# Two transformer layers on one core: what is asked for first, and where the memory rows and bias rows stand

## The chip, the cores and the metric

The kernel runs on one core of a Trainium2 chip. The metric is the device time of one execution in microseconds (us), median of three runs. The engines named below are PE (matrix products), DVE (vector), ACT (scalar/activation), POOL (general) and SP (which here only asks for transfers). PE writes into 8 banks of an accumulator memory (`PS`); DVE and ACT read from it.

## The reference

Two layers over a sequence of 512 rows of width 1024. Only the start of layer one matters here:

```
h = rmsnorm(x, g_pre_mix)                       # x: 512 x 1024
proj = h @ w_in                                 # columns: cb, cc, cv, q, k, v, qm, ga, gb, gc
o = moba_attention(q, k, v, rel_bias)           # logits + bias by distance (32 buckets, 8 heads), softmax, @ v
y_c = memory_attention(qm, rmsnorm(mem, g_mem), w_mem_kv)   # mem: 256 x 1024
merged = sigmoid(ga) * y_a + sigmoid(gb) * y_b + sigmoid(gc) * y_c
x = x + rmsnorm(merged @ w_out); then a gated feed-forward part; then layer two (state space, attention, experts)
```

The norm of `x` comes before every product; the norm of `mem` is first used by the product `mk` (behind `q`, `k`, `v`). The bias by distance is first used by the logits of the attention.

## The kernel before

Each engine has one program, written in the order in which it runs; engines wait for each other on counters. Nothing is reordered by a planner, so the order in the code is the order on the engine.

**Weights.** `weight_plan` cuts the weights into chunks of 1 MB ([128, 2048] f32), two of them (`q` half 0 and 1) for the name `q`, two for `k` and so on. Chunks are numbered here 0, 1 (`q`), 2, 3 (`k`), 4, 5 (`v`), 6, 7 (`mk`). There are two landing places: chunk n may only be asked for when chunk n-2 has been emptied. A chunk of these names has two parts of width 1024; part 0 and 1 lie in chunk 0, part 2 and 3 in chunk 1, and so on. Each part is split in a high and a low half: ACT makes the high half (`one_hi`, L1919, fed by `highs`), DVE the low half (`one_lo`, L1109, fed by `lows`); a chunk is empty when the low half of its last part is made. A product of two such pairs takes three matmuls (L490, L491, L492). `upto(e, n)` makes all parts below n that aren't made yet; `ahead(name, j)` makes up to the part four behind the start of tile j. The high half of part i also waits until the tile of part i-4 has been computed. SP's program asks for chunks (`one_in`, L2568) in order, each as soon as its place is empty.

**The head.** SP asks for `x` in four blocks of 512 KB (L2579) and then for chunks 0 and 1. ACT asks for four tables (`cols`, `consts`, `rows`, `wsmall`, L2078 to L2081), POOL for the memory rows `mem` (L2404, 2 x 512 KB), `onehot` and `rel_bias`. For each 128 rows ACT takes the sum of squares (`squared`, L1928), POOL turns it into a scale (`norm`: L2370, then L2373, which needs `consts`), DVE scales the rows (`scaled`, L1119). PE turns the scaled rows (`turned`, L486: one bank for each of 8 column groups, N1 for `x`, NM for `mem`), ACT writes the high half (L1935) and DVE the low half (L1129).

In before the order on ACT is: squares of x (4), squares of mem (2), high halves of parts 0 to 3, turned N1, turned NM, `q` tiles. On DVE: scale x (4), scale mem (2), low halves of parts 0 to 3, turned N1, the bias copy (L1337, L1339), turned NM, `q` tiles. On PE: turned N1, the bias product (L705), turned NM, four `q` tiles, four `k` tiles, the `v` rows, then attention.

**Bias.** The bias product gives 8 rows of 512. When DVE has copied them to `BV`, POOL writes each 128 times to DRAM (`bvec`, L2412, 2.5 MB), asks for `gains`, and then reads skewed rows back (`skew`, L2421) for the logits.

**Banks.** `banks.take` hands out the 8 banks in turn; who takes one waits for whoever last read it.

Of the kernel before, what the change touches and what calls it, by code (L numbers as in the profile page):

```python
# [175 lines left out]
class Events:  # L176
# [12 lines left out]
    def tick(self, name, key=0, by=1):  # L189
        self.n[name] = self.n.get(name, 0) + by  # L190
        if self.made:
            assert self.value[name, key] == self.n[name], (name, key)
            return self.sem(name), by
        assert (name, key) not in self.value, (name, key)
        self.value[name, key] = self.n[name]
        return None, by

    def at(self, name, key=0):
        return (self.sem(name), self.value[name, key]) if self.made else (name, 0)
# [59 lines left out]
def two_layers(nc, dram, out):  # L259
    ctx = ExitStack()  # L260
    with ctx:
# [43 lines left out]
        def ps(key):  # L305
            return PS[:, banks.of.get(key, 0), :]
# [170 lines left out]
        def tensor(e):  # L477
            def turned(N, consts=False):
                for k in range(8):
                    b, was = banks.take((N.name, k), ("v_out", (N.name, "l", k)))  # L480
                    if was:
                        e.wait_ge(*at(*was))
                    e.wait_ge(*at("consts"))
                    for i in range(N.n):
                        e.wait_ge(*at("v_out", (N.name, "x", i)))
                        m = e.i.transpose(PS[:, b, 128 * i:128 * i + 128], N.xn[:, i, 128 * k:128 * k + 128], ident)  # L486
                    m.then_inc(*tick("acc", (N.name, k)))
# [6 lines left out]
            def tile(name, j, N, back, n=512):  # L494

                b, was = banks.take((name, j), back)
                if was:
                    e.wait_ge(*at(*was))
                e.wait_ge(*at("w_lo", (name, j)))
                wh, wl = (cut(w, 8) for w in halves(name, j))  # L500
                for k in range(8):
                    e.wait_ge(*at("v_out", (N.name, "l", k)))
                    m = product(PS[:, b, 0:n], (wh[:, k, :], wl[:, k, :]), (N.hi[k], N.lo[k]), k == 0, k == 7)
                m.then_inc(*tick("acc", (name, j)))
# [193 lines left out]
                tile(name, j, N3, ("v_out", ("cs", tix, 3)))  # L698

            turned(N1)  # L700
            b, was = banks.take("bias", ("v_out", "bv"))
            e.wait_ge(*at(*was)) if was else None
            e.wait_ge(*at("onehot"))
            e.wait_ge(*at("rel_bias"))
            e.i.matmul(PS[0:8, b, :], GB[0:32, 512:520], GB[0:32, 0:512], start=True, stop=True).then_inc(*tick("acc", "bias"))  # L705
            turned(NM)
            for name in ("q", "k"):
                for j in range(4):
                    tile(name, j, N1, ("v_out" if j % 2 else "a_out", (name, j)))
            rows("v", N1, 4, lambda i: ("a_out", ("v", i)))  # L710
            zipped(attention_1(), dense_1())
            for bi in (1, 2):
# [391 lines left out]
        def vector(e):  # L1104
# [12 lines left out]
            def scaled(N, i):  # L1117
                e.wait_ge(*at("p_out", (N.name, "r", i)))
                e.i.tensor_scalar(N.xn[:, i, :], N.src[:, i, :], N.ss(i), None, ALU.mult).then_inc(  # L1119
                    *tick("v_out", (N.name, "x", i)))  # L1120
# [17 lines left out]
            def projected(name, dst):  # L1138
                for j in range(4):
                    projected_one(name, j, dst)  # L1140
# [189 lines left out]

            for i in range(4):
                scaled(N1, i)
            for i in range(2):
                scaled(NM, i)
            lows.upto(e, 4)
            turned(N1)
            e.i.memset(BV[0:8, 512:640], NEG).then_inc(*tick("v_out", "neg"))  # L1337
            e.wait_ge(*at("acc", "bias"))
            e.i.tensor_copy(BV[0:8, 0:512], ps("bias")[0:8, :]).then_inc(*tick("v_out", "bv"))  # L1339
            turned(NM)  # L1340
            projected("q", QT)
            projected("k", KT)
            for u in range(4):
                ahead("v", u)
# [567 lines left out]
        def scalar(e):  # L1912
# [14 lines left out]
            def squared(N, i):  # L1927
                e.i.activation(N.xn[:, i, :], N.src[:, i, :], ACT.Square, accum_out=N.ss(i)).then_inc(  # L1928
                    *tick("a_out", (N.name, "s", i)))
# [14 lines left out]
            def projected(name, dst):  # L1944
                for j in range(4):
                    projected_one(name, j, dst)
# [131 lines left out]
            e.i.dma_start(CP, dram["cols"]).then_inc(*tick("cols", 0, 16))  # L2078
            e.i.dma_start(CC, dram["consts"]).then_inc(*tick("consts", 0, 16))
            e.i.dma_start(RR, dram["rows"].to_broadcast([128, NROW])).then_inc(*tick("rows", 0, 16))  # L2080
            e.i.dma_start(WS, dram["wsmall"]).then_inc(*tick("wsmall", 0, 16))  # L2081


            for i in range(4):
                e.wait_ge(*at(f"xin{i}"))
                squared(N1, i)
            for i in range(2):
                e.wait_ge(*at(f"mem{i}"))
                squared(NM, i)
            highs.upto(e, 4)  # L2090
            turned(N1)
            turned(NM)
            projected("q", QT)
            projected("k", KT)
            for u in range(4):
                ahead("v", u)
# [271 lines left out]
        def pool(e):  # L2368
# [31 lines left out]
                    norm(N, i)  # L2400


            for i in range(2):
                e.i.dma_start(MEMR[:, i, :], dram["mem"][128 * i:128 * i + 128, :]).then_inc(*tick(f"mem{i}", 0, 16))  # L2404
            e.i.dma_start(GB[0:32, 0:512], dram["onehot"]).then_inc(*tick("onehot", 0, 16))
            e.i.dma_start(GB[0:32, 512:520], dram["rel_bias"]).then_inc(*tick("rel_bias", 0, 16))
            for i in range(4):
                norm(N1, i)
            for i in range(2):
                norm(NM, i)  # L2410
            e.wait_ge(*at("v_out", "bv"))
# [151 lines left out]
        def sync(e):  # L2563
            def one_in(e, n):
                c = chunks[n]
                for was in c.free:
                    e.wait_ge(*at(*was))
                e.i.dma_start(area(c.place, 2048), dram["wpack"][SLOT[c.name], :, 2048 * c.half:2048 * c.half + 2048]).then_inc(  # L2568
                    *tick(f"w_in{c.slot}", n, 16))

            loads = Feed(one_in)

            def until(name, j):

                p = parts[PART[name, j] + 3]
                loads.upto(e, CHUNK[p.chunk.name, p.chunk.half] + 3)

            for i in range(4):
                e.i.dma_start(X[:, i, :], dram["x"][128 * i:128 * i + 128, :]).then_inc(*tick(f"xin{i}", 0, 16))  # L2579
            until("down4", 3)  # L2580
            e.wait_ge(*at("acc", ("n3", 7)))
            e.i.dma_start(WD, dram["wdt"]).then_inc(*tick("wdt", 0, 16))
            loads.upto(e, len(chunks))

            def gates_in(n):


                e.wait_ge(*at("acc", ("gu", n // 2 - 3) if n > 5 else ("oo", 3, 1)))
                if n == 5:
                    e.wait_ge(*at("v_out", "wts"))  # L2590
                    e.wait_ge(*at("v_out", "be"))
                w, n_ = area(GUs[n % 6], 4096), 4096 if n < 2 * END else 2048
                e.i.dma_start(w[:, 0:n_], wexp[n, :, 0:n_]).then_inc(*tick(f"gu{n % 6}", n, 16))

            def rest_in(n):
                w = area(GUs[n % 6], 4096)
                e.i.dma_start(w[:, 2048:4096], wexp[n, :, 2048:4096]).then_inc(*tick(f"gu_rest{n % 2}", 0, 16))

            def downs_in(n):
                if n > 5:  # L2600
                    e.wait_ge(*at("acc", ("dn2", n // 2 - 3, 1)))
                e.i.dma_start(area(DNs[n % 6], 2048), wexp[n, :, 4096:6144]).then_inc(*tick(f"dn{n % 6}", n, 16))

            for blk in range(NBLK):
                n, m = 2 * blk, 2 * blk + 1
                if blk == 2:

                    gates_in(n)
                    downs_in(n)
                    downs_in(m)  # L2610
                    gates_in(m)
                    continue
                gates_in(n)
                gates_in(m)
                if blk == END:
                    rest_in(n)
                    rest_in(m)
                downs_in(n)
                downs_in(m)
            overflow(e, sync_more, before_end)  # L2620
            for s in range(2):
                e.wait_ge(*at(f"scatter{s}", END - 1 - s))
            e.wait_ge(*at("acc", ("gu", END - 2)))
            for i in range(4):
                e.i.dma_start(YC[i], YA2[128 * i:128 * i + 128]).then_inc(*tick(f"yc{i}", 0, 16))
            for i in range(4):
                e.wait_ge(*at("v_out", ("oc", i, 1)))
                e.i.dma_start(out[128 * i:128 * i + 128, :], X[:, i, :]).then_inc(*tick(f"out{i}", 0, 16))
            for i in range(4):
                e.wait_ge(*at(f"out{i}"))  # L2630
# [260 lines left out]
```

## Time and profile before

| | us |
|---|---|
| median of 3 runs | 2213.04 (2212.13 to 2213.21) |
| profiled execution | 2212.32 |
| its span | 2210.2 |
| PE busy | 2021.2 (91%) |
| DVE busy | 993.7 (45%) |
| ACT busy | 699.5 (32%) |
| POOL busy | 218.8 (10%) |
| mean granted clock of PE | 0.969 |

The span is what the hardware profiler recorded from the first to the last instruction; the profiled execution took 2.1 us more than that. PE busy at 91% is a mean over stages: in the first 100 us of the span it stands still before the first product and is dense behind it.

### The profile page before, as it was taken

Reading aid. Unit: us, or ns where it says so; the run is one execution under the profiler, and the core shown is the slowest. Engines: PE = TensorE matmul, PEld = TensorE weight load, DVE = VectorE, ACT = ScalarE, POOL = GpSimd, SP = SyncE. Lnnn points to the kernel's source line nnn. Section 1 sums busy time; section 2 is a strip of 40 time slices with the busy share of each in tenths; the row PEclk is TensorE's granted clock in tenths of the full one; section 3 lists DMA queues with packets and bytes.
Section 4 is the critical chain, followed back from the end, with each engine's and each line's share of the span. In section 5 each row is a group of like instructions: output and inputs, shape, how many; then the busy total and the mean of one; then the engine's idle time right before and its main releaser. Section 6 shows DMA issues by size and latency. Waiting matters only on the chain.

```text
span 2210.2 us, 23020 instructions
## 1 busy us (share of the span) xinstructions
PE 2021.2 (91%) x9514; PEld 1406.4 (64%) x9514; DVE 993.7 (45%) x1558; ACT 699.5 (32%) x1120; POOL 218.8 (10%) x280
## 2 busy tenths in 40 slices
PE   6989999997999999899999999999995988888886
PEld 4867788896888788777777765666693332322232
DVE  4366534335666622668887426662236111111113
ACT  4343323324444412555554322552121110100100
POOL 1000000002000000101211102110023111111110
PEclk9999999998999999999999999999997999999999
DMA  6531223242222332232232222112229999999995
GB/s 188 137 129 62 76 77 108 83 153 105 96 96 95 111 118 95 105 124 68 91 115 95 91 76 77 58 58 76 77 96 368 413 423 423 424 424 420 417 414 224
DMA packets 57336, 380.42 MB, mean 172 GB/s; under 512 B 13424, under 2 KB 13680, under 8 KB 24336
## 3 DMA queue, kind: packets, MB, share of 16 engines
q1 hardware_dynamic: 38304, 339.23, 39.4%
q0 software_dynamic: 18352, 38.66, 5.7%
q8 instruction: 75, 1.23, 0.2%
q10 hardware_dynamic: 576, 1.05, 0.1%
q14 instruction: 29, 0.24, 0.0%
HBM read 376.20 MB, written 27.86 MB: 183 GB/s over the span
## 4 chain that ended last, share of the span: by engine, by line
PE 69%; DMA 18%; DVE 8%; ACT 3%; issue 1%; POOL 1%; SPq 0%; DVEq 0%; POOLq 0%; ACTq 0%
PE PS L490 17%; PE PS L492 16%; PE PS L491 16%; DMA AR<-in_wexp 16%; PE PS L1067 4%; PE PS L860 4%; PE PS L537 2%; DVE rf L1109 2%; DVE AR L1326 1%; PE PS L841 1%; ACT rf L1919 1%; PE PS L486 1%; PE PS L1090 1%; PE PS L893 1%; PE PS L925 1%
## 5 line engine op out<-in xcount | busy, mean ns | idle before, releaser
L490 PE MATMUL PS<-rf,rf 128*128 128x512 f32 (+1 forms) x1896 | 725.8, 383 | 18.2 <-DVE rf L1109 10.7
L492 PE MATMUL PS<-rf,rf 128*128 128x512 f32 (+1 forms) x1896 | 713.7, 376 | 0.0
L491 PE MATMUL PS<-rf,rf 128*128 128x512 f32 (+1 forms) x1896 | 713.0, 376 | 0.0
L1109 DVE TENSOR_TENSOR rf<-AR,rf 128x1024 fp32r<-128x1024 f32 (+1 forms) x210 | 268.4, 1285 | 396.1 <-ACT rf L1919 396.1
L490 PEld LDWEIGHTS PS<-rf,rf 128*128 128x128 f32 x1896 | 360.9, 190 | 91.4 <-issue 18.0
L491 PEld LDWEIGHTS PS<-rf,rf 128*128 128x128 f32 x1896 | 361.1, 190 | 64.9 <-issue 3.1
L492 PEld LDWEIGHTS PS<-rf,rf 128*128 128x128 f32 x1896 | 360.0, 190 | 64.3
L1919 ACT ACTIVATE rf<-AR 128x1024 fp32r<-128x1024 f32 (+1 forms) x210 | 229.0, 1101 | 304.6 <-PE PS L492 191.4
L1067 PE MATMUL PS<-AR 128*64 128x512 f32 x1024 | 267.6, 629 | 54.9 <-DMA AR<-in_wexp 53.2
L1067 PEld LDWEIGHTS PS<-AR 128*64 128x64 f32 x1024 | 82.0, 145 | 234.8 <-issue 157.6
L1864 DVE TENSOR_TENSOR AR<-AR,PS 128x256 f32<-128x256 f32 x32 | 13.5, 422 | 358.9 <-ACT AR L2359 358.9
L1090 PE MATMUL PS<-AR 128*64 128x512 f32 x512 | 116.9, 599 | 16.5 <-DVE AR L1868 16.5
L860 PE MATMUL PS<-AR 128*128 128x512 f32 x256 | 112.5, 595 | 0.0
L2359 ACT ACTIVATE AR<-PS 128x256 f32<-128x256 f32 x32 | 12.3, 383 | 296.7 <-PE PS L1067 296.7
L1090 PEld LDWEIGHTS PS<-AR 128*64 128x64 f32 x512 | 33.9, 137 | 79.0 <-issue 54.8
L860 PEld LDWEIGHTS PS<-AR 128*128 128x128 f32 x256 | 47.9, 190 | 56.8 <-issue 56.2
L1326 DVE SCALAR_TENSOR_TENSOR AR<-PS,AR 128x511 f32<-128x511 f32 (+2 forms) x72 | 53.8, 747 | 13.8 <-ACT AR L2071 12.1
L2516 POOL DMA_INDIRECT AR<-h2d,IA x32 | 32.7, 1022 | 272.1 <-PE PS L1076 252.4
L2365 ACT ACTIVATE AR<-PS 128x512 f32<-128x512 f32 x32 | 19.1, 597 | 127.0 <-PE PS L1090 127.0
L486 PE MATMUL PS<-AR 128*128 128x128 f32 x112 | 24.7, 382 | 36.6 <-DVE AR L1119 36.4
L537 PE MATMUL PS<-AR 128*128 128x512 f32 x128 | 56.2, 592 | 0.0
L1872 DVE COPY AR<-PS 128x512 f32<-128x512 f32 x32 | 22.1, 692 | 65.3 <-PE PS L1090 65.3
(324 smaller groups left out, 1826.2 us busy)
## 6 DMA issues: line engine op xcount, KB each, us to landing
AR<-in_wexp SPq DMA_DIRECT2D x62, 2048.0 KB, 35.9
AR<-in_wpack SPq DMA_DIRECT2D x123, 1024.0 KB, 5.1
AR<-in_wexp SPq DMA_DIRECT2D x68, 1024.0 KB, 38.1
AR<-acud POOLq DMA_DIRECT2D x16, 512.0 KB, 4.0
AR<-ya SPq DMA_DIRECT2D x4, 1024.0 KB, 8.1
bvec<-AR POOLq DMA_DIRECT2D x1, 2560.0 KB, 54.8
AR<-in_x SPq DMA_DIRECT2D x4, 512.0 KB, 8.3
AR<-bvec POOLq DMA_DIRECT2D x8, 256.0 KB, 3.0
```

What stands on the lines that cost most here:

```text
L486: m = e.i.transpose(PS[:, b, 128 * i:128 * i + 128], N.xn[:, i, 128 * k:128 * k + 128], ident)
L490: e.i.matmul(o, ws[0], xs[0], start=start, stop=False)
L491: e.i.matmul(o, ws[0], xs[1], start=False, stop=False)
L492: return e.i.matmul(o, ws[1], xs[0], start=False, stop=stop)
L537: m = e.i.matmul(PS[:, b, :], w[:, k, c:c + 128], src[:, k, :], start=k == 0, stop=k == kt - 1)
L860: m = e.i.matmul(PS[:, b, :], w[:, d, :], YT[:, d, :], start=d == 0, stop=d == 15)
L1067: m = e.i.matmul(PS[CAP * j:CAP * j + CAP, b, :], xt[:, k, CAP * j:CAP * j + CAP], w[:, k, :], start=k == 0, stop=k == 7)
L1090: m = e.i.matmul(PS[CAP * j:CAP * j + CAP, b2[hf], :], hd[:, q, CAP * j:CAP * j + CAP], w[:, q, 512 * hf:512 * hf + 512], start=q == 0, st ...
L1109: e.i.tensor_tensor(rounded(p.place + p.width, p.width), src, rounded(p.place, p.width).bitcast(F32), ALU.subtract).then_inc(*tick("w_lo", ...
L1326: e.i.scalar_tensor_tensor(out=y[:, q:512], in0=b[:, 0:512 - q], scalar=cp("conv_w", 24 * (3 - q) + tix), in1=y[:, q:512], op0=ALU.mult, o ...
L1919: e.i.activation(rounded(p.place, p.width), area(p.chunk.place + p.off, p.width), ACT.Copy).then_inc(*tick("w_hi", p.key))
L2516: e.i.indirect_dma_start(XB[:, s, :], None, dram["h2d"], bass.IndirectOffsetOnAxis(ap=IA[:, 128 + blk:129 + blk], axis=0), bounds_check=51 ...
```

## The change

- SP: x, then only chunk 0; chunk 1 is asked for when all four blocks of x have landed.
- ACT: `wsmall` and the squares of mem move behind turned N1; of the parts only part 0 is split before turned N1, parts 1 and 2 behind it.
- DVE: only part 0 is split before turned N1, part 1 behind it; the scaling of mem moves behind the `q` tiles 0 and 1; turned NM behind tile 3.
- POOL: `mem` is asked for behind the four norms of x.
- PE: turned N1, `q` tile 0, the bias product, `q` tiles 1 to 3, turned NM, `k`.

```diff
@@ PE
             turned(N1)
-            b, was = banks.take("bias", ("v_out", "bv"))
-            (waits for onehot and rel_bias, the bias matmul)
-            turned(NM)
             for name in ("q", "k"):
                 for j in range(4):
                     tile(name, j, N1, ("v_out" if j % 2 else "a_out", (name, j)))
+                    if name == "q" and j == 0:
+                        b, was = banks.take("bias", ("v_out", "bv"))
+                        (waits for onehot and rel_bias, the bias matmul)
+                if name == "q":
+                    turned(NM)
@@ DVE
             for i in range(4):
                 scaled(N1, i)
-            for i in range(2):
-                scaled(NM, i)
-            lows.upto(e, 4)
+            lows.upto(e, 1)
             turned(N1)
+            lows.upto(e, 2)
             e.i.memset(BV[0:8, 512:640], NEG).then_inc(*tick("v_out", "neg"))
             e.wait_ge(*at("acc", "bias"))
             e.i.tensor_copy(BV[0:8, 0:512], ps("bias")[0:8, :]).then_inc(*tick("v_out", "bv"))
+            projected_one("q", 0, QT)
+            projected_one("q", 1, QT)
+            for i in range(2):
+                scaled(NM, i)
+            projected_one("q", 2, QT)
+            projected_one("q", 3, QT)
             turned(NM)
-            projected("q", QT)
             projected("k", KT)
@@ ACT
             e.i.dma_start(RR, dram["rows"].to_broadcast([128, NROW])).then_inc(*tick("rows", 0, 16))
-            e.i.dma_start(WS, dram["wsmall"]).then_inc(*tick("wsmall", 0, 16))
             for i in range(4):
                 e.wait_ge(*at(f"xin{i}"))
                 squared(N1, i)
+            highs.upto(e, 1)
+            turned(N1)
+            highs.upto(e, 3)
+            e.i.dma_start(WS, dram["wsmall"]).then_inc(*tick("wsmall", 0, 16))
             for i in range(2):
                 e.wait_ge(*at(f"mem{i}"))
                 squared(NM, i)
-            highs.upto(e, 4)
-            turned(N1)
+            projected("q", QT)
             turned(NM)
-            projected("q", QT)
             projected("k", KT)
@@ POOL
-            (mem: two DMAs)
             (onehot, rel_bias)
             for i in range(4):
                 norm(N1, i)
+            (mem: two DMAs)
             for i in range(2):
                 norm(NM, i)
@@ SP
             for i in range(4):
                 e.i.dma_start(X[:, i, :], dram["x"][128 * i:128 * i + 128, :]).then_inc(*tick(f"xin{i}", 0, 16))
+            loads.upto(e, 1)
+            for i in range(4):
+                e.wait_ge(*at(f"xin{i}"))
             until("down4", 3)
```

On DVE, at the start of its program, with the counters that an instruction waits for; this is before. TENSOR_SCALAR scales rows, TENSOR_TENSOR into `rf_1024` is the low half of a part, SCALAR_TENSOR_TENSOR the low half of a turned group (512 wide for x, 256 for mem), the copy of 8x512 is the bias, a copy of 128x512 a `q` or `k` tile with an odd number.

```order
L1119 TENSOR_SCALAR AR<-AR 128x1024 [waits s_p_out] x6
L1109 TENSOR_TENSOR rf_1024<-AR,rf_1024 128x1024 [waits s_w_hi] x4
L1129 SCALAR_TENSOR_TENSOR rf_1536<-PS,AR,rf_1536 128x512 [waits s_a_out] x8
L1337 MEMSET AR 8x128
L1339 COPY AR<-PS 8x512 [waits s_acc]
L1129 SCALAR_TENSOR_TENSOR rf_1536<-PS,AR,rf_1536 128x256 [waits s_a_out] x8
```

The same place of the changed kernel:

```order
L1122 TENSOR_SCALAR AR<-AR 128x1024 [waits s_p_out] x4
L1112 TENSOR_TENSOR rf_1024<-AR,rf_1024 128x1024 [waits s_w_hi]
L1132 SCALAR_TENSOR_TENSOR rf_1536<-PS,AR,rf_1536 128x512 [waits s_a_out] x8
L1112 TENSOR_TENSOR rf_1024<-AR,rf_1024 128x1024 [waits s_w_hi]
L1339 MEMSET AR 8x128
L1341 COPY AR<-PS 8x512 [waits s_acc]
L1112 TENSOR_TENSOR rf_1024<-AR,rf_1024 128x1024 [waits s_w_hi] x3
L1139 COPY AR<-PS 128x512 [waits s_acc]
L1122 TENSOR_SCALAR AR<-AR 128x1024 [waits s_p_out] x2
L1112 TENSOR_TENSOR rf_1024<-AR,rf_1024 128x1024 [waits s_w_hi] x2
L1139 COPY AR<-PS 128x512 [waits s_acc]
L1132 SCALAR_TENSOR_TENSOR rf_1536<-PS,AR,rf_1536 128x256 [waits s_a_out] x8
```

Two scalings and three low halves left the place ahead of the turned x. The bias copy now stands ahead of the low halves of parts 2 and 3 (first two of the x3), and the low halves of parts 5 and 6 ahead of the copy of `q` tile 3 and of the turned mem.

On ACT, before, from the last squares on; an ACTIVATE into `rf_1024` is the high half of a part, one from `PS` into `rf_1536` a turned group, one from `PS` into `AR` the copy of an even tile. `s_w_in0` and `s_w_in1` are the landings of even and odd chunks.

```order
L1928 ACTIVATE AR<-AR 128x1024 [waits s_mem1]
L1919 ACTIVATE rf_1024<-AR 128x1024 [waits s_w_in0]
L1919 ACTIVATE rf_1024<-AR 128x1024 [waits s_w_in1]
L1935 ACTIVATE rf_1536<-PS,AR 128x512 [waits s_acc] x7
L1935 ACTIVATE rf_1536<-PS,AR 128x256 [waits s_acc] x8
L1942 ACTIVATE AR<-PS 128x512 [waits s_acc]
```

And now, from the squares of mem on:

```order
L1935 ACTIVATE AR<-AR 128x1024 [waits s_mem1]
L1926 ACTIVATE rf_1024<-AR 128x1024
L1949 ACTIVATE AR<-PS 128x512 [waits s_acc]
L1926 ACTIVATE rf_1024<-AR 128x1024 [waits s_w_in0]
L1926 ACTIVATE rf_1024<-AR 128x1024 [waits s_acc]
L1949 ACTIVATE AR<-PS 128x512 [waits s_acc]
L1926 ACTIVATE rf_1024<-AR 128x1024 [waits s_w_in1]
L1942 ACTIVATE rf_1536<-PS,AR 128x256 [waits s_acc] x8
```

Between the squares and the turned mem now stand parts 3 to 6 and two copies; the last of these parts (part 6) is the first of chunk 3 and waits for its landing.

## Rows read from the trace of the kernel before

**Rows 1.** Chain that ended last, 0 to 34 us: start, us, what.
```profile
2.11 12.89 DMA AR<-in_x
...
20.80 4.54 DVE rf L1109 x4
25.34 2.65 DVE rf L1129 x4
```

**Rows 2.** Windows A:B: us, busy (xstarts) PE PEld DVE ACT POOL, PEclk, DMA share, GB/s.
```profile
31.70:34.80 3.10, 3.10 (x9) 2.48 (x8) 2.71 (x7) 0.64 (x2) 1.61 (x2) 0.51 0.31 29
...
55.20:77.00 21.80, 21.80 (x98) 18.07 (x97) 4.88 (x5) 4.15 (x5) 0.00 (x0) 1.00 0.61 129
77.00:99.00 22.00, 22.00 (x102) 18.01 (x102) 6.55 (x6) 7.12 (x9) 1.07 (x2) 1.00 0.64 191
```

**Rows 3.** Timeline, 0 to 60 us: start, us, engine, line, what [idle before <-releaser].
```profile
9.40 0.58 POOL L2373 TENSOR_TENSOR AR<-AR 128x1 f32<-128x1 f32 x1 [3.23 <-DMA AR<-in_consts]
10.02 0.75 DVE L1119 TENSOR_SCALAR AR<-AR 128x1024 f32<-128x1024 f32 x1 [10.02 <-POOL AR L2373]
...
11.49 0.76 DVE L1119 TENSOR_SCALAR AR<-AR 128x1024 f32<-128x1024 f32 x1 [0.72 <-POOL AR L2373]
...
17.11 0.75 DVE L1119 TENSOR_SCALAR AR<-AR 128x1024 f32<-128x1024 f32 x1 [2.58 <-POOL AR L2373]
...
17.92 4.92 PE L486 MATMUL PS<-AR 128*128 128x128 f32 x29 [2.86 <-DVE AR L1119]
...
26.05 1.02 PE L705 MATMUL PS<-AR 32*8 32x512 f32 x2 [3.22 <-DVE rf L1129]
...
30.67 0.61 DVE L1339 COPY AR<-PS 8x512 f32<-8x512 f32 x1
...
31.58 1.17 POOL L2412 DMA_DIRECT2D bvec<-AR  x1 [11.57 <-DVE AR L1339]
```

**Rows 4.** DMA queues, 0 to 15.1 us: packets, MB, share of 16 engines.
```profile
q1 hardware_dynamic: 627, 2.52, 44.4%
q0 software_dynamic: 352, 1.12, 21.4%
q10 hardware_dynamic: 571, 1.05, 20.8%
```

**Rows 5.** SP's timeline, 24 to 26, 42 to 50 and 73 to 76 us.
```profile
25.41 0.33 SPq L2568 DMA_DIRECT2D AR<-in_wpack  x1
46.75 0.33 SPq L2568 DMA_DIRECT2D AR<-in_wpack  x1
74.37 0.33 SPq L2568 DMA_DIRECT2D AR<-in_wpack  x1
```

**Rows 6.** DMA, 42 to 50 us: queues as in rows 4; issues: KB each, us to landing.
```profile
q0 software_dynamic: 80, 0.41, 48.4%
q1 hardware_dynamic: 39, 0.32, 14.3%
...
AR<-in_wpack SPq DMA_DIRECT2D x1, 1024.0 KB, 23.5
```

**Rows 7.** DMA queues, 52 to 58 us, and 64 to 68 us.
```profile
q0 software_dynamic: 59, 0.30, 47.5%
...
q0 software_dynamic: 39, 0.20, 32.0%
q1 hardware_dynamic: 38, 0.31, 18.3%
```

**Rows 8.** Timeline of DVE, ACT and POOL, 55 to 95 us.
```profile
55.24 0.69 DVE L1136 COPY AR<-PS 128x512 f32<-128x512 f32 x1 [2.64 <-PE PS L492]
70.24 2.01 ACT L1919 ACTIVATE rf<-AR 128x1024 fp32r<-128x1024 f32 x2 [8.96 <-DMA AR<-in_wpack]
86.62 1.07 POOL L2421 DMA_DIRECT2D AR<-bvec  x2 [53.30 <-DMA bvec<-AR]
90.09 2.01 ACT L1919 ACTIVATE rf<-AR 128x1024 fp32r<-128x1024 f32 x2 [9.79 <-DMA AR<-in_wpack]
```

More of the change, by code:

```diff
@@ L700, in tensor @@
             turned(N1)
-            b, was = banks.take("bias", ("v_out", "bv"))
[L702 to L705, printed above, removed]
-            turned(NM)
             for name in ("q", "k"):
@@ L709, in tensor @@
                     tile(name, j, N1, ("v_out" if j % 2 else "a_out", (name, j)))
+                    if name == "q" and j == 0:
+                        b, was = banks.take("bias", ("v_out", "bv"))
+                        e.wait_ge(*at(*was))
+                        e.wait_ge(*at("onehot"))
+                        e.wait_ge(*at("rel_bias"))
+                        e.i.matmul(PS[0:8, b, :], GB[0:32, 512:520], GB[0:32, 0:512], start=True, stop=True).then_inc(
+                            *tick("acc", "bias"))
+                if name == "q":
+                    turned(NM)
             rows("v", N1, 4, lambda i: ("a_out", ("v", i)))
@@ L2400, in norm_add @@
                     norm(N, i)
-            for i in range(2):
-                e.i.dma_start(MEMR[:, i, :], dram["mem"][128 * i:128 * i + 128, :]).then_inc(*tick(f"mem{i}", 0, 16))
             e.i.dma_start(GB[0:32, 0:512], dram["onehot"]).then_inc(*tick("onehot", 0, 16))
@@ L2408, in pool @@
                 norm(N1, i)
+            for i in range(2):
+                e.i.dma_start(MEMR[:, i, :], dram["mem"][128 * i:128 * i + 128, :]).then_inc(*tick(f"mem{i}", 0, 16))
             for i in range(2):
```

## The prediction

> **What bounds the kernel now.** I read the page, the chain of waits of the first 34 us, the timeline and the windows of the first 100 us, and last the DMA view in short stretches. The chain begins with 12.9 us in which the last block of x lands, at 15.0 [rows 1]; 1 MB of mem rows, two chunks of weights and four tables are asked for beside it. Then come the norms, four low halves on DVE (4.5 us) and the turned groups at 0.66 us each. The first `q` tile starts at 31.7. From there PE has no gap up to 99 us, so whatever brings the `q` and `k` tiles forward shortens the kernel by as much, as long as nothing else is late. Its first 3.1 us run at half clock (0.51, 9 matmuls, against 98 in 21.8 us behind it [rows 2]). A tile of 24 matmuls at full clock is 21.8 / 4 = 5.45 us; the copy of `q` tile 3 at 55.24 [rows 8] marks its end, so `k` tile 0 starts at about 55.05 (a copy starts 0.2 us behind the last matmul). Counting back three tiles, `q` tile 0 took 31.7 to 38.9, 7.2 us, 1.7 us of it the slow clock.
>
> **x lands earlier.** Up to 15.1 us the queues took 44.4% (SP), 21.4% (POOL) and 20.8% (ACT), together 13.1 us of the engines' time [rows 4]. Of POOL's 1.12 MB, 1.05 are mem rows and go behind: 3.0 us less. Of ACT's 1.05 MB, 0.29 are `wsmall`: 0.28 x 3.1 = 0.9 us less. SP moved 2.52 MB where x is 2.10, the rest a piece of chunk 0 that may still come between (0 to 1.1 us; I take 0.6). Last block of x: 15.0 - 3.0 - 0.9 - 0.6 = 10.5, bounds 9.9 to 11.1. The last scaling starts 2.1 us behind the landing (17.11), that is 12.6; but the scalings follow each other at 1.47 us (10.02, 11.49) from the landing of `consts` on, at 9.4 [rows 3], which I put at 8.1 by the same shares: 8.7 + 3 x 1.47 = 13.1. I take the later. Transposes 0.8 later, at 13.9, and 4.9 us of them: `q` tile 0 can start at 18.8.
>
> **What must be ready by then.** Chunk 0 follows x on SP's queue, 1.05 MB at about 400 GB/s (4.68 MB in 15.1 us is 310, with small packets among them): landed at about 13; its high half 1.05 us [rows 8], its low half (4.54 / 4 and a gap, 1.2) until 15.3, then DVE's turned groups at 0.66 until 20.7. The tile needs the last group at 18.8 + 4.8 = 23.6, so 2.9 us of cover. Part 1's halves come behind the turned groups (by 22) and are wanted at 25.2. There is no gap ahead of tile 0 now, so I expect it at full clock: end 24.3. The bias product takes 1.0 [rows 3]: 25.2. Tiles 1 to 3: end at 41.6. The squares and scalings of mem (1.05 us each on ACT, 0.75 on DVE) lie beside these tiles. So tile 3 ends 13.5 us earlier than before; the turned mem (16 transposes at the 29-in-4.9 us rate or better, plus one copy before its last bank is free) adds 2.1 and `k` tile 0 would start at 43.7, 11.4 us earlier. That is the gain if nothing new is late.
>
> **What is new and late.** The bias copy on DVE now waits for tile 0 and ends at 25.9; before it ended at 31.3. The write of `bvec` follows 0.3 us behind it [rows 3], and takes to 86.6 [rows 8], 53 us. The low halves of parts 2 and 3 now stand *behind* that copy: 2 x 1.2 us, done at 28.3. Only then is chunk 1 empty and chunk 3 asked for (SP issued it 0.07 us behind the last low half before: 25.41 against 25.34 [rows 1, 5]). Before, chunk 3 was on its way 6 us ahead of `bvec`; now it comes 2.1 us behind it. The one chunk asked for well inside `bvec` in these rows, chunk 4 at 46.75 [rows 5], took 23.5 us to land [rows 6], and ACT did wait for it up to 70.24 [rows 8]. `bvec` keeps half of the DMA engines full (48.4%, 80 packets in 8 us [rows 6]). The free half took its share of chunk 4 quickly (0.32 MB by 50 [rows 6]); from 52 to 58 SP's queue moved nothing at all though the chunk was outstanding; at 64 to 68 the two queues go packet for packet (39 and 38) [rows 7]. 39 packets on 8 engines in 4 us make 0.82 us for one of each; a chunk of 8 KB packets has 8 for each engine, 6.6 us, and with 1.3 us ahead of the first packet and 1 us for the landing, 23.5 leaves 14.6 us in which a full engine did nothing for it. I read that as work of `bvec` which the engine had already taken in, and which it takes in soon after `bvec` begins. No row shows a chunk that meets the first 2 us of `bvec`, so the bounds are no stand at all (landing at 37) and a stand until `bvec` is over (82); I take the one measured, 23.5.
>
> Chunk 3 then lands at 28.3 + 23.5 = 51.8. ACT has its part 6 *ahead of* the turned mem: high half to 52.9 (two take 2.01 [rows 8]). DVE has part 6's low half ahead of the copy of tile 3: to 54.1, copy to 54.8. PE's last turned mem group takes the bank of tile 3 and waits for that copy, and `k` tile 0 takes the bank of the first mem group and waits for DVE's low half of it. `k` tile 0: 55.3, against 55.05. PE stands still from about 43 to 55 and its clock falls, as it did behind the pause of 3.2 us ahead of the bias product [rows 3], after which the window at 31.7 has 0.51 [rows 2]: 1.6 us at the start of `k`, as then. Sum: +0.25 + 1.6 = +1.9 us. The 11.4 us are spent waiting for chunk 3.
>
> Beyond it: chunk 5 is asked for at about 59.5, and by 20 to 24 us lands at 80 to 83, where the third `v` part is wanted at 55.3 + 1.6 + 21.8 + 10.9 = 89.6. `bvec` ends 5 us earlier (81) and its readers run with attention, which starts later than before. PE had no gap from 77 to 99 [rows 2], so the 1.9 us stay. The profiled execution took 2212.32 us, so it would be 2214.2; the median of the runs is 0.7 above it: 2214.9.
>
> The Trainium skill, page DMA: Bandwidth & Descriptors, section Queues, rings and completion order, says that each DMA engine takes turns between the queues that have work, a packet at a time. The trace agrees at 64 to 68 us and not at 52 to 58. By that rule chunk 3 would not stand at all, which is the first rival.
>
> **Rivals.**
> A. Chunk 3 isn't held up, because so shortly after its start `bvec` has not filled the engines, or holds it up for less. With turns from the start it lands at 28.3 + 1.3 + 6.6 + 1 = 37.2. Part 6 is ready by 39.5, tile 3 ends at 41.6, nobody waits: -11.4, 2201.6. For it: the turns at 64 to 68, and 2 us is little. Against: 52 to 58. Between a landing at 39 and one at 52 each us costs one, so the gain is over 0.2% up to a landing at about 45.
> B. On the other side: the held half of chunk 3 is served only when `bvec` is over, as chunk 6 was: asked for at 74.37 [rows 5], landed at 90.1 [rows 8], behind the end of `bvec` at 86.6. `bvec` from 28 to 78 (80 packets of 5 KB in 8 us are 0.41 MB [rows 6], so 2.6 MB take 51 us alone), chunk 3 at 82, `k` tile 0 at 85.5: +30 + 1.6, 2245. It costs more than 4.4 us as soon as the stand is 3 us longer than chunk 4's. Against: chunk 4 was being served by 64 [rows 7], with 22 us of `bvec` left.
> C. x lands hardly earlier (SP's queue is the limit): then everything shifts by up to 3 us, bvec and chunk 3 too, and since the landing of chunk 3 hangs on tile 0's end it is +2 to +5: 2215 to 2218.
>
> **Chances.** Forecast (landing at 49 to 54): 0.52, own range 2212 to 2218. A 0.33, half of it near 2202 and half between 2203 and 2209. B 0.05. C and late landings beyond 54: 0.10. A measurement here can't tell less than 0.2% (4.4 us) from no change. Faster by more: A, 0.33. Slower by more: B, half of C and the top of the forecast, 0.13. Same: 0.54. The range reaches down to A and leaves out B: 2200 to 2219.
>
> **What would show it.** Right: last block of x at 10 to 11; `q` tile 0 starting at 18 to 20 with the granted clock at 1.0; chunk 3 asked for at about 28 and landed near 52, ACT waiting on `in_wpack` for 10 us or more ahead of the turned mem; PE idle from 43 to 55, the clock at 0.5 behind it. Wrong: a `k` tile 0 that starts at 44, with ACT's part 6 near 39 (A), or at 80 (B); a `q` tile 0 at half clock; a tile that waits for chunk 1 or 2 or for `consts`.

## The result and the profile after

The changed kernel takes 2216.14 us (median of 15 runs, 2214.73 to 2218.91), the kernel before 2212.15 us beside it (15 runs). The ratio is 1.0017, 95% interval [1.0009, 1.0025]: 3.8 us slower, interval 2.0 to 5.5. The forecast was 1.9 us slower with "the same" as the likeliest case. The waits foretold for it are all there; their sizes are off by up to 2 us.

The chain of waits of the changed kernel, 0 to 60 us (start, us, what); it answers to [rows 1]. `AR` is the on-chip array of plain values, `rf` that of the high and low halves.

```profile
2.11 9.45 DMA AR<-in_x
11.58 1.16 ACT AR L1935 x2
...
14.62 6.09 PE PS L486 x29
...
26.20 0.97 PE PS L709 x2
27.18 0.68 DVE AR L1341
27.86 2.28 DVE rf L1112 x2
30.21 23.13 DMA AR<-in_wpack
53.36 1.07 ACT rf L1926
54.45 1.23 DVE rf L1112
55.68 0.61 DVE AR L1139
56.33 0.69 PE PS L486 x2
57.02 0.50 PE PS L490
```

x is in at 11.56 instead of 15.0, and `q` tile 0 starts at 20.5 instead of 31.7. Then one transfer, chunk 3, asked for at 30.21 behind the bias copy and the two low halves, takes 23.13 us and is the chain. High half, low half, copy of tile 3, last turned mem group, `k` tile 0: each step follows the one before within 0.1 us.

The timeline of PE and POOL (start, us, engine, line, what, idle before and releaser):

```profile
43.53 1.69 PE L486 MATMUL PS<-AR 128*128 128x128 f32 x14
56.33 0.69 PE L486 MATMUL PS<-AR 128*128 128x128 f32 x2 [11.11 <-DVE AR L1139]
56.73 0.80 PE L490 MATMUL PS<-rf,rf 128*128 128x512 f32 x1
...
28.16 1.17 POOL L2421 DMA_DIRECT2D bvec<-AR  x1 [1.76 <-DVE AR L1341]
84.23 1.08 POOL L2430 DMA_DIRECT2D AR<-bvec  x2 [54.33 <-DMA bvec<-AR]
```

PE turns 14 of 16 mem blocks and then stands 11.1 us for the copy of tile 3. `k` tile 0 starts at 56.7, 1.7 us later than before (55.05). Two windows of the same kernel (us, busy and starts of PE, PEld, DVE, ACT, POOL, granted clock, DMA share, GB/s) show the clock, as [rows 2] did:

```profile
20.50:26.20 5.70, 5.70 (x27) 4.45 (x26) 3.13 (x5) 5.70 (x9) 1.29 (x4) 1.00 0.45 111
56.70:61.40 4.70, 4.70 (x13) 3.67 (x12) 3.84 (x8) 1.69 (x3) 0.00 (x0) 0.52 0.51 109
```

`q` tile 0 runs at full clock (before it began at half); the slow stretch has moved to the start of `k` and is longer: 13 matmuls in 4.7 us. From the start of `k` tile 0 to attention (first L583) it takes 102.53 - 56.73 = 45.8 us, before 98.65 - 55.05 = 43.6. So attention starts 3.9 us later: 1.7 by the wait and 2.2 by the clock. That agrees with the 4.0 us between the two medians. It is not carried to the end unchanged: matched instruction by instruction on DVE, the two profiles are 4.8 us apart at 150 us, 1.0 at 990 and 4.7 at the end.

### The profile page after: what moved, and what is told of

Same layout as the page of the kernel before. It is cut to its first block, busy times and chain, and to the rows that moved or that the text cites. A ratio compares the mean times of both kernels' runs of the same rounds, so it can differ in the third digit from the quotient of the medians.

```text
span 2214.9 us, 23019 instructions
## 1 busy us (share of the span) xinstructions
PE 2024.8 (91%) x9514; PEld 1407.8 (64%) x9514; DVE 993.5 (45%) x1558; ACT 699.6 (32%) x1120; POOL 218.7 (10%) x280
## 4 chain that ended last, share of the span: by engine, by line
PE 68%; DMA 18%; DVE 8%; ACT 3%; issue 1%; POOL 1%; SPq 0%; DVEq 0%; POOLq 0%; ACTq 0%
PE PS L490 16%; PE PS L491 16%; PE PS L492 16%; DMA AR<-in_wexp 16%; PE PS L1070 5%; PE PS L863 4%; PE PS L537 2%; DVE rf L1112 2%; DVE AR L1329 2%; ACT rf L1926 1%; DMA AR<-in_wpack 1%; PE PS L844 1%; PE PS L486 1%; PE PS L1093 1%; PE PS L896 1%
## 5 line engine op out<-in xcount | busy, mean ns | idle before, releaser
L490 PEld LDWEIGHTS PS<-rf,rf 128*128 128x128 f32 x1896 | 360.3, 190 | 92.2 <-issue 18.9
L2367 ACT ACTIVATE AR<-PS 128x256 f32<-128x256 f32 x32 | 12.3, 384 | 298.3 <-PE PS L1070 298.3
L863 PEld LDWEIGHTS PS<-AR 128*128 128x128 f32 x256 | 47.8, 190 | 56.9 <-issue 56.3
L486 PE MATMUL PS<-AR 128*128 128x128 f32 x112 | 22.4, 367 | 44.2 <-DVE AR L1122 33.1
L1329 DVE SCALAR_TENSOR_TENSOR AR<-PS,AR 128x511 f32<-128x511 f32 (+2 forms) x72 | 53.8, 747 | 12.8 <-ACT AR L2078 11.1
```

The lines of the kernel that those rows point to most:

```text
L490: e.i.matmul(o, ws[0], xs[0], start=start, stop=False)
L863: m = e.i.matmul(PS[:, b, :], w[:, d, :], YT[:, d, :], start=d == 0, stop=d == 15)
L1329: e.i.scalar_tensor_tensor(out=y[:, q:512], in0=b[:, 0:512 - q], scalar=cp("conv_w", 24 * (3 - q) + tix), in1=y[:, q:512], op0=ALU.mult, o ...
```

## Experiments

Theory: chunk 3 is late because `bvec` holds it up, and its lateness reaches PE through the order on ACT and DVE. Rival 1: it is late since it is asked for late. Rival 2: the new place of the turned mem on PE costs the time. Every run is compared with the kernel before on the same chip. The yardsticks in the traces are the start of `k` tile 0 (before 55.05, changed 56.73) and of attention (98.65, 102.53).

**bvec behind chunk 3.** The changed kernel, with one more wait on POOL (`gains`, 512 KB, stands behind `bvec` in POOL's order and moves with it):

```diff
             e.wait_ge(*at("v_out", "bv"))
+            e.wait_ge(*at("w_in1", 3))
             e.i.dma_start(dram["bvec"], ...)
```

> The changed kernel, with one more wait on POOL: bvec is written only when chunk 3 has landed. Chunk 3 is asked for at the same time (30.2 us). Theory (bvec's traffic holds chunk 3 up): chunk 3 lands near 35 instead of 53.3, k tile 0 starts near 46 at full clock instead of 56.7, some 13 us gained; bvec itself ends 7 us later, near 91, and the logits that need it at about 91 wait some 4 to 6 us, so 2206 to 2210 us in all. Rival 1 (chunk 3 is late because it is asked for late, whatever else runs): it lands at 50 or later, no gain, 2216 or more. Rival 2 (the place of the turned mem on PE and its banks cost the time, chunk 3 is a bystander): chunk 3 lands early and k tile 0 still starts near 56.

2213.9 us (10 runs), ratio to before 1.0008 [0.9998, 1.0017]. Chunk 3, asked for at 30.01, landed 5.1 us later (DMA issues, 28 to 34 us: KB, us to landing), and `k` tile 0 started at 44.99:

```profile
AR<-in_wpack SPq DMA_DIRECT2D x1, 1024.0 KB, 5.1
```

Rivals 1 and 2 fall: asked for at the same time, without `bvec` and `gains`, the chunk is on time, and the turned mem stands where it stood. But only 2.2 us of the 11.7 arrived, fewer than the 6 to 10 expected. The timeline of ACT and of PE says why:

```profile
95.21 1.06 ACT L1926 ACTIVATE rf<-AR 128x1024 fp32r<-128x1024 f32 x1 [13.21 <-DMA AR<-in_wpack]
96.17 2.04 ACT L2107 ACTIVATE AR<-PS 128x512 f32<-128x512 f32 x4
...
97.38 4.58 PE L583 MATMUL PS<-AR 64*128 64x128 f32 x16 [8.58 <-ACT AR L2107]
```

`bvec`, now from 35.9 to 91.9, held an `mk` chunk up instead. ACT has that chunk's part ahead of the `v` copies, and the attention on PE waits for the banks that they free: 8.6 us, and the clock falls again (16 matmuls in 4.58 us against 2.43). I had looked for the wait at the readers of `bvec`; it was a wait for a chunk again, the second of `mk` (chunk 7, asked for at 76.33). The chunks from 5 on were late in this run, 23.1, 21.4 and 18.9 us to landing. Chunk 4 was not: asked for at 35.86, while `bvec` was issued at 35.85, it landed after 5.3 us.

**Parts 2 and 3 split ahead of the bias copy.** DVE stood 3.3 us there waiting for the bias product.

```diff
@@ DVE
-            lows.upto(e, 2)
+            lows.upto(e, 4)
             e.i.memset(BV[0:8, 512:640], NEG).then_inc(*tick("v_out", "neg"))
@@ ACT
-            highs.upto(e, 3)
+            highs.upto(e, 4)
             e.i.dma_start(WS, dram["wsmall"]).then_inc(*tick("wsmall", 0, 16))
```

> The changed kernel, with parts 2 and 3 split ahead of the bias copy (DVE stood 3.3 us waiting for the bias product there) and part 3's high half ahead of the squares of mem. Theory: chunk 3 is asked for near 26 instead of 30.2, moves ahead of bvec's first packets (30.2) and lands near 31; bvec is not later. k tile 0 starts near 46 at full clock, attention near 89: 13 us less than the changed kernel, 2203 us. Rival 1 (asked for late, at the pace of 23 us): lands at 49, 4 us gained, 2212. Rival 2 (turned mem and banks): no gain, 2216.

2204.13 us (5 runs), ratio to before 0.9959 [0.9946, 0.9973]: 12 us less than the changed kernel. Chunk 3 was asked for at 25.77, still ahead of `bvec` (POOL at 27.79), and landed at 33.6:

```profile
AR<-in_wpack SPq DMA_DIRECT2D x1, 1024.0 KB, 7.8
...
43.16 1.91 PE L486 MATMUL PS<-AR 128*128 128x128 f32 x16
44.82 0.47 PE L490 MATMUL PS<-rf,rf 128*128 128x512 f32 x1
...
89.91 2.43 PE L583 MATMUL PS<-AR 64*128 64x128 f32 x16 [1.28 <-ACT AR L2107]
```

The mem blocks are turned in one piece, `k` starts at 44.8 and attention at 89.9. So 4.4 us earlier in the request made 15.3 us less in the transfer's duration. This version beats both kernels.

**Part 6 behind the turned mem.** The transfers stay; ACT and DVE no longer wait for chunk 3 in front of the turned mem.

```diff
@@ DVE
             projected_one("q", 2, QT)
-            projected_one("q", 3, QT)
+            e.wait_ge(*at("acc", ("q", 3)))
+            e.i.tensor_copy(QT[:, 3, :], ps(("q", 3))).then_inc(*tick("v_out", ("q", 3)))
             turned(NM)
@@ ACT
-            projected("q", QT)
+            for j in range(3):
+                projected_one("q", j, QT)
             turned(NM)
```

> The changed kernel, with the halves of part 6 moved behind the turned mem on ACT and DVE; transfers as they were. Theory: chunk 3 still lands near 53, but only k tile 2 needs it, at 56.8; k tile 0 starts near 46 at full clock, PE has no pause, 13 us gained, 2203 us. Rival 1 (only the transfer counts, wherever its halves stand): the pause moves to k tile 2 and stays 10 us long, 2214 to 2216. Rival 2 (turned mem and banks): k tile 0 still at 56, 2216.

2211.98 us (11 runs), ratio 0.9997 [0.9988, 1.0006]: 4.2 us less than the changed kernel, where 13 were expected. `k` tile 0 did start at 44.88, so the way from chunk 3 to PE was the order on ACT and DVE, as the theory has it. The rest went to later chunks (timeline of ACT, then PE):

```profile
53.59 2.01 ACT L1927 ACTIVATE rf<-AR 128x1024 fp32r<-128x1024 f32 x2 [6.93 <-DMA AR<-in_wpack]
61.41 2.01 ACT L1927 ACTIVATE rf<-AR 128x1024 fp32r<-128x1024 f32 x2 [5.33 <-DMA AR<-in_wpack]
80.81 2.00 ACT L1927 ACTIVATE rf<-AR 128x1024 fp32r<-128x1024 f32 x2 [16.91 <-DMA AR<-in_wpack]
...
83.18 0.79 PE L490 MATMUL PS<-rf,rf 128*128 128x512 f32 x1 [5.10 <-DVE rf L1112]
```

A chunk asked for inside `bvec` still takes its 20 us or more; PE, earlier now, runs into the one for `v` and stands 5.1 us, with its clock down behind it (it granted half in the window from 81.3 to 83.2, before PE went on). Attention starts at 96.5. Rival 1 was right that the lateness comes out elsewhere, wrong on the place and the size.

**The requests alone.** The kernel before, with the edits of the change on SP and POOL and `wsmall` behind the squares of x, no order of the computing changed:

```diff
@@ SP
+            loads.upto(e, 1)
+            for i in range(4):
+                e.wait_ge(*at(f"xin{i}"))
             until("down4", 3)
@@ POOL
-            (mem: two DMAs)
             (onehot, rel_bias; norm(N1, 0) to norm(N1, 3))
+            (mem: two DMAs)
```

> The kernel before, with the order of the requests alone changed (chunk 1 behind x, mem behind the norms of x, wsmall behind the squares of x); the order of the computing stays. Theory: x is in at 11.6 instead of 15.0, but ACT's squares of mem stand ahead of the split and wait for mem, which is asked for at 13.7 and lands near 20; the turned x moves from 22 to about 26 on ACT: 4 us slower than before, 2216. Rival (the early x alone carries a gain): 3 us faster, 2209.

2216.71 us (10 runs), ratio 1.0019 [1.001, 1.0028]; attention starts at 101.58. As expected: ACT stands for the mem rows ahead of everything else.

```profile
11.51 1.06 ACT L1928 ACTIVATE AR<-AR 128x1024 f32<-128x1024 f32 x1 [0.47 <-DMA AR<-in_x]
20.81 1.06 ACT L1928 ACTIVATE AR<-AR 128x1024 f32<-128x1024 f32 x1 [8.15 <-DMA AR<-in_mem]
```

**The order alone.** The changed kernel with the requests put back as before (the reverse of the last diff, on SP, POOL and ACT).

> The changed kernel with the requests as the kernel before has them (mem, wsmall and chunk 1 at once); the order of the computing stays changed. Theory: the last block of x lands at 15.0 instead of 11.6, tile 0, the bias copy, bvec and the request for chunk 3 all move by 2.5 to 3.5 us, and since chunk 3 stands behind bvec as long as before, so does everything else: k tile 0 near 59.5 to 60, 2219. Rival (the pause up to 56 is fixed in time by the transfer, so an earlier x only makes it longer): no change, 2216.

2220.23 us (5 runs), ratio 1.0035 [1.0022, 1.0048]: 4.1 us above the changed kernel. Chunk 3 was asked for at 33.49, took 23.2 us, and `k` started at 60.08, 3.35 us later than in the changed kernel. The early x is worth its 3.4 us and passes them on, since everything behind hangs on tile 0 by a fixed sum. Neither half of the change is a gain by itself.

**bvec over 16 engines.** The changed kernel; the 8 rows go to DRAM first and are copied from there by a transfer whose outermost dimension is 128.

```diff
-            e.i.dma_start(dram["bvec"], BV[0:8, 0:640].unsqueeze(1).to_broadcast([8, 128, 640])).then_inc(
+            e.i.dma_start(dram["x1d"][0:8, 0:640], BV[0:8, 0:640]).then_inc(*tick("bvrow", 0, 16))
+            e.wait_ge(*at("bvrow"))
+            e.i.dma_start(bass.AP(dram["bvec"].tensor, 0, [[640, 128], [81920, 8], [1, 640]]),
+                          bass.AP(dram["x1d"].tensor, 0, [[0, 128], [1024, 8], [1, 640]])).then_inc(
                 *tick("bvec", 0, 16))
```

> The changed kernel, with bvec made in two steps: the 8 rows (20 KB) are stored to DRAM and from there copied 128 times by one transfer whose outermost dimension is 128 instead of 8. Theory: it is the half of the engines that the one long transfer fills for 50 us which holds chunks up; spread over all, at the 400 GB/s of the start it takes some 7 to 10 us, chunk 3 (asked for at 30.2) lands near 38 and k tile 0 starts near 45; later chunks land in 5 us, attention near 89 without the waits seen with bvec behind chunk 3 (8.6 us on PE). 2202 us. Rival (any 2.5 MB beside the chunks cost as much): chunk 3 lands later than 45, 2208 or more.

2203.74 us (5 runs), ratio 0.996 [0.9946, 0.9974]: 12.4 us less than the changed kernel. First the queues from 33 to 40 us, then the issue (KB, us to landing), then PE:

```profile
q0 software_dynamic: 378, 1.94, 97.5%
...
bvec<-x1d POOLq DMA_DIRECT2D x1, 2560.0 KB, 17.5
...
44.21 0.48 PE L490 MATMUL PS<-rf,rf 128*128 128x512 f32 x1
...
87.93 2.43 PE L583 MATMUL PS<-AR 64*128 64x128 f32 x16
```

The same bytes now fill all engines (97.5% against 48% before [rows 6]) for a short time: 17.5 us to landing instead of 54 to 56. ACT's waits for `in_wpack` in the first 100 us add up to 3.4 us, against 27.1 in the changed kernel, and PE stands nowhere up to attention at 87.9. The duration was longer than the 7 to 10 us expected.

For chunk 3 this run does not show what the spreading is worth, since the edit turned the order of the two requests round as well. The copy waits for the 8 rows to reach DRAM, and x was turned 0.9 us faster here (5.17 us). So chunk 3 was asked for ahead of it (timelines of SP and of POOL) and landed in 5.2 us at 34.4, where 38 had been expected:

```profile
29.23 0.33 SPq L2580 DMA_DIRECT2D AR<-in_wpack  x1
...
29.40 0.94 POOL L2423 DMA_DIRECT2D bvec<-x1d  x1 [1.62 <-DMA x1d<-AR]
```

What the spreading does shows in the later chunks. Chunk 4, asked for at 35.09 inside the copy, took 12.3 us against 25.0 in the changed kernel, and those behind it 4.8 to 5.1. A chunk 3 behind the spread copy was not run; with the 12.3 us of chunk 4 it would land near 42.5 and `k` start near 46 (my estimate). Source and layout of the copy changed together (DRAM for on-chip rows, 128 outermost for 8), and no run tells them apart.

**The kernel before with bvec over 16 engines.** The same edit on the kernel before.

> The kernel before with bvec in two steps over all engines. Theory: PE had no gap from 31.7 to 99 us, chunks were late but covered, so nothing is gained up to attention: 2212, within 1 us. Rival (bvec's traffic costs time in the kernel before too, by contention somewhere): 3 us or more gained.

2212.71 us (11 runs), ratio 1.0 [0.9991, 1.0009]; attention at 98.84. In the kernel before, the slow transfer is fully covered: it costs only once the head is faster.

**Both cures.** Early split and `bvec` over 16 engines.

> Both cures together: parts 2 and 3 split ahead of the bias copy and bvec over all engines. Theory: they take away the same wait, so together they give little more than either: k tile 0 near 44.8 as with the early split, attention at 88.5 instead of 89.9, since the 1.3 us that PE waited there for the v copies go too: 2202 to 2203. Rival (two separate costs): the gains add up, 2195.

2204.33 us (5 runs), ratio 0.9964 [0.995, 0.9978]; `k` at 45.08, attention at 88.80. They don't add up: each of them alone already gets chunk 3 asked for ahead of the long transfer. The three fast versions can't be told apart in time.

## Why the prediction was right, and where it was off

- **x earlier: right, 1 us too much.** 11.56 instead of the 10.5 forecast (bounds 9.9 to 11.1), so outside its bounds. The DMA queues from 0 to 11.6 us (packets, MB, share of 16 engines) tell which terms were off:

```profile
q1 hardware_dynamic: 620, 2.46, 58.9%
q10 hardware_dynamic: 432, 0.76, 22.3%
q0 software_dynamic: 64, 0.07, 1.8%
```

  POOL's queue gave back its 3.0 us. ACT's went from 3.1 to 2.6 us, 0.55 less and not 0.9. SP's went from 6.7 to 6.8, 0.1 more and not 0.6 less: about as much of chunk 0 as before still came between. Together 3.4 us, as measured, and not 4.5.
- **Start of tile 0: 20.5 instead of 18.8.** The last scaling starts at 13.81 (13.1 forecast), 0.7 us of the 1.7. It hung on the landing of x (2.25 us behind it), where I had let the pace of the scalings from `consts` on decide. The rest is the 29 transposes, 6.09 us against 4.92 before [rows 3]. Runs with the same order up to there had 5.2 to 6.2 us for them, the requests put back 6.10; what slows them was not followed.
- **Full clock for tile 0: right** (1.00 from 20.5 to 26.2).
- **Cover for chunk 0, part 1 and the turned groups: right.** No tile waited for them. The mem rows were covered too.
- **bvec ahead of chunk 3: right.** POOL issued at 28.16, SP at 30.21, a distance of 2.05 us (2.1 forecast).
- **The duration of chunk 3: right,** 23.1 us against 23.5 taken over from chunk 4. That was the step on which forecast and rival A parted, and a chunk that meets the first 2 us of `bvec` stands as long as one asked for 15 us behind its issue. Rival A (turns from the start) has no place here: with it chunk 3 would have landed at 39. What it would have been worth, the early split shows, where the chunk lands at 33.6: 2204. The queues of the changed kernel from 41 to 44 us, and from 46 to 51:

```profile
q0 software_dynamic: 30, 0.15, 48.7%
...
q0 software_dynamic: 47, 0.24, 33.4%
q1 hardware_dynamic: 45, 0.37, 17.4%
```

  From 41 to 44 SP's queue (q1) moved nothing, though chunks 3 and 4 were outstanding; from 46 on the two queues went packet for packet. The Trainium skill, page DMA: Bandwidth & Descriptors, section Queues, rings and completion order, says that an engine takes turns between queues and drains a whole packet, typically 9 to 17 descriptors, in each. The prediction left that number out and took a turn for one of the profile's packets, so its "would not stand at all" is not what the page says. With 0.78 us for one write of `bvec` (48.4% of 16 engines for 8 us, 80 packets [rows 6]) such a turn would be 7 to 13 us, an estimate from the page's figure. The trace agrees with neither reading throughout: some 14 us without service on the engines of `bvec`, then turns of one packet.
- **The way to PE: right,** shown by moving part 6 alone (`k` at 44.9).
- **The slow clock behind the pause: sized 1.6 us, measured 2.2.** I took the loss of `q` tile 0 before, but there the half clock had begun earlier and its first part had fallen on the turned mem (window 28.0 to 31.7 of the kernel before):

```profile
28.00:31.70 3.70, 3.67 (x12) 1.73 (x12) 3.70 (x8) 2.52 (x6) 0.12 (x1) 0.50 0.53 206
```

  So the 3.2 us pause before was followed by 6.8 us at half clock (27.9 to 34.8). In the changed kernel PE works at half clock from 56.3 to 61.2, 4.8 us. Behind the pauses of 5.1, 8.6 and 11.2 us in the other runs it was 4.7, 4.4 and 4.8 us, so a longer pause did not cost more. (Counted back by three tiles of 5.45, `q` tile 0 ended at 38.7 and not 38.9; the 1.6 us in the sum are right for it.)
- **The sum:** +0.25 for the wait was +1.7, +1.6 for the clock was +2.2. The terms that failed in size are the landing of x and the transposes, together 1.7 us (less 0.4 that chunk 3 took under its 23.5), handed on without loss by the chain from tile 0 to chunk 3, as the run with the requests put back shows for 3.4 us. 1.9 us forecast, 3.8 measured.
- **What I had not seen:** that the hold of `bvec` on *later* chunks would take most of the gain back as soon as `k` comes early. I had checked the third `v` part only in the forecast's own timing and not in rival A's, and the `v` copies behind an `mk` part not at all. The two runs with 8.6 and 5.1 us of PE's waiting show both.

Attention starts 8.7 us earlier with the early split and 10.7 with 16 engines, 9.9 with both, while the three medians differ by under 1 us. From `k` to attention it takes 45.1 us with the early split and 43.7 in the other two, the 1.3 us that PE waits for the `v` copies; the start of `k` (44.8, 44.2, 45.1) follows the transposes of x (5.8, 5.2, 6.2 us). Behind attention, matched on DVE, the lead with 16 engines falls from 11.1 to 8.2 us between 987 and 1011 us, in layer two. But the kernel before with 16 engines, whose head is as before, falls from 1.1 ahead to 1.9 behind at the same place. So these 3 us are not the head's; what they are is open.

Open too is what inside an engine keeps a new chunk standing; that it is work already taken in fits, but is only argued. And no run tells `bvec` from `gains` right behind it; from 41 to 44 us q0's packets were 5 KB each, those of `bvec`.

## What to carry to other kernels

A transfer that fills half of the DMA engines for 50 us is harmless while every load is asked for well ahead, and can become the bound when the head gets faster: look at what a request meets on its way, not only at how early it is made. When a copy that releases such a transfer moves past the step that releases the next load, compare the order of the two issues; 4.4 us decided over 15 here. And a step that waits for a load must not stand ahead of work on the same engine that others wait for.

## What was unexpected of the hardware

- A chunk took 5.1 us to land alone, 7.8 when asked for 2.0 us ahead of `bvec`, 5.3 when asked for together with it, 23.1 when 2.05 us behind it and 23.5 when 15 us behind it [rows 3, 5, 6]: no gradual rise.
- Behind the spread copy there was a stand too, a shorter one: 12.3 us for a chunk asked for 5.7 us behind its issue.
- A 2.5 MB store from 8 partitions took 54 to 56 us, the same bytes DRAM to DRAM, outermost dimension 128, 14.2 to 17.5 us.
- The pause of 11.1 us on PE cost another 2.2 us through the granted clock, and PE's work at half clock was 4.4 to 4.8 us long behind pauses of 5.1 to 11.2 us.
